# Rounded-weight products of gate and up first, remainder products behind them, in a transformer kernel

## The chip, the cores and the metric

One core of a Trainium2 chip runs the whole program. The metric is the device time of one execution in microseconds (us), the median of three runs. TensorE (PE in the profile, PEld for its weight loads) multiplies, VectorE (DVE) and ScalarE (ACT) work on tiles, GpSimd (POOL) does small things, SyncE (SP) issues nearly all DMAs. The engines have one instruction stream each and wait for one another on semaphores.

## The reference, cut to what matters

The reference is a chain of two transformer stacks of two layers each over 256 tokens of width 1024, all in float32. Between attention parts it has six feed-forward blocks (one in each layer of the first stack, two in each layer of the second), all of this form, with a hidden width of 2816:

```
def swiglu(x, wg, wu, wd):
    return (jax.nn.silu(x @ wg) * (x @ wu)) @ wd
```

## The kernel before, in words

Every weight matrix is read from memory in units of 1 MB (128 partitions by 2048 float32). There are three buffers of each kind, so unit u uses buffer u mod 3. For each unit SP fills `raw` (L562), ACT writes the rounded weights `w_hi` (`split_hi`, L761) and counts `hi_ready`, DVE writes what rounding lost, `w_lo = raw - w_hi` (`split_lo`, L1178), and counts `lo_ready`. A product in nearly full precision is then made of products with `w_hi` and with `w_lo`. When PE is done with a unit it counts `unit_used`; ACT may write `w_hi` of unit u+3 only when unit u is counted, and SP may refill `raw` when `w_lo` of its former unit is written.

A feed-forward block (`ffn`, f = 0 to 5) works through 11 groups of 256 hidden columns. Each group has three units: gate (G), up (U) and down (D). For a gate or an up unit PE runs `wide` (L1992): 16 matmuls of 512 columns with rounded weights (`rounded`, L2006; both halves of the split activations at once), then 16 of 256 columns with the remainders (`remainder`, L2010), into a pair of PSUM banks, G_B for gate and U_B for up. A down unit (`down`, L2043) is 24 matmuls of 512 columns (helper `three`, L1907 to L1909) into four other banks. PE's order is G, U of group g+1, then D of group g; only at the end of a block D9 and D10 stand one right behind the other, behind U10.

What ACT and DVE do with a group, in their order in a steady group (`group` L862, and DVE's `gates` and `group` around L1241 to L1262):

- ACT: `split_hi` of the down unit; `split_hi` of the next gate unit (waits for G counted); `gate_sum` copy of half of G_B (L861); silu (L868); `up_sum` copy of half of U_B (L870, waits for U counted); `hid_hi` (L872, the rounded hidden values); `split_hi` of the next up unit.
- DVE: `split_lo` of the down unit; `gate_sum` addition (L1238, after which G_B is free); multiplication of the gate sums (L1246); `split_lo` of the next gate unit; `up_sum` addition (L1253, after which U_B is free); product `hid` (L1257); `hid_lo` (L1260, what rounding of the hidden values lost); `split_lo` of the next up unit.

PE's D of group g waits for `hid_lo` of group g (`hidden_lo`). In the last group the place of the next gate unit is taken by unit D10, the place of the next up unit by the first unit of the next stage (unit 33 of the block), and the second unit of the next stage (34) follows. The last block loads none of those two.

Behind a block stands either an addition to x in halves by DVE (`add_ffn`, L1613; blocks 2, 3 and 4), then transposes on PE that wait for it (`turn_piece`, L1880); or a norm with squares on ACT, products on DVE (L1589, L1228) and transposes (L1896; blocks 0 and 1); or the final norm (block 5). L1866 are matmuls without use, which only keep PE busy. The first group of a block is made by `wide_first` and `wide` called directly; `gate_up` makes groups 1 to 10.

The diff touches `gate_up` alone.

Of the kernel before, what the change touches and what calls it, by code (L numbers as in the profile page):

```python
# [29 lines left out]
KC = D // P  # L30
# [210 lines left out]
def build(nc, a, noted):  # L241

    with ExitStack() as ctx:
# [91 lines left out]
        G_B, U_B, ACC = pair[0], pair[1], bank[4:8]  # L335
# [87 lines left out]
        def sem(name):  # L423
            return ctx.enter_context(nc.semaphore(name))

        def sig(name):
# [3 lines left out]
        hi_ready, lo_ready, unit_used = sem("hi_ready"), sem("lo_ready"), sem("unit_used")  # L430
# [3 lines left out]
        gate_cross, up_cross, gate_summed, up_summed = (  # L434
            sem(n) for n in ("gate_cross", "up_cross", "gate_summed", "up_summed"))
# [87 lines left out]
        def hi_half(which, c):  # L523
            return which[:, 2 * SEQ * c:2 * SEQ * c + SEQ]
# [1337 lines left out]
        def _(pe):  # L1862
# [120 lines left out]
            def ffn(f, pieces):  # L1983
                u0 = ffns[f][0]
                base = NG * f

                def split_weights(u):

                    s = u % RING
                    return [v[s][:, :].rearrange("p (c n) -> p c n", c=KC) for v in (w_hi, w_lo)]  # L1990

                def wide(u, i, out):  # L1992

                    pe.wait_ge(hi_ready, u + 1 + 6 * i)
                    w = split_weights(u)
                    for c in range(KC):
                        for m in range(2):
                            rounded(w, out, m, c)
                    pe.wait_ge(lo_ready, u + 1 + 6 * i)
                    for c in range(KC):  # L2000
                        for m in range(2):
                            last = remainder(w, out, m, c)
                    return last

                def rounded(w, out, m, c):
                    pe.matmul(out[:, 512 * m:512 * (m + 1)], w[0][:, c, P * m:P * (m + 1)],  # L2006
                              xt[:, 2 * SEQ * c:2 * SEQ * (c + 1)], start=(c == 0), stop=False)

                def remainder(w, out, m, c):
                    return pe.matmul(out[:, 512 * m + SEQ:512 * (m + 1)], w[1][:, c, P * m:P * (m + 1)],  # L2010
                                     hi_half(xt, c), start=False, stop=(c == KC - 1))
# [23 lines left out]

                def gate_up(u, i, g):

                    pe.wait_ge(gate_summed, base + g)
                    wide(u, i, G_B).then_inc(unit_used, 1)
                    pe.wait_ge(up_summed, base + g)  # L2040
                    wide(u + 1, i, U_B).then_inc(unit_used, 1)

                def down(u, i, g, p, first, last_group):  # L2043
                    s = u % RING
# [22 lines left out]
                pe.matmul(ACC[0][:, 0:SEQ], ones[:, :], rstd_diag, start=True, stop=True)\  # L2067
                  .then_inc(small_mm.sem, small_mm.mark(("rstd rows", f)))
                gate_up(u0 + 2, 0, 1)
                pe.wait_ge(prep_ready.sem, prep_ready.at(("rstd rows", f)))  # L2070
                down(u0 + 4, 0, 0, 0, True, False)
                with pe.Fori(0, 4) as i:
                    for j in range(2):
                        gate_up(u0 + 5 + 3 * j, i, 2 * i + j + 2)
                        down(u0 + 7 + 3 * j, i, 2 * i + j + 1, 1 - j, False, False)
                gate_up(u0 + 29, 0, 10)
                down(u0 + 31, 0, 9, 1, False, False)
                down(u0 + 32, 0, 10, 0, False, True)
# [186 lines left out]
            u = 0  # L2265
# [192 lines left out]
```

## Time and profile before

| | |
|---|---|
| median of 3 runs | 1627.94 us (1627.82 to 1628.86) |
| profiled execution | 1628.18 us, of which the span of the program 1626.3 us |
| granted clock of TensorE | 0.999 of full |
| PE busy | 1602.4 us (99%) |
| PE weight loads busy | 1362.1 us (84%) |
| DVE busy | 1068.3 us (66%) |
| ACT busy | 881.3 us (54%) |
| POOL busy | 85.4 us (5%) |
| mean DMA rate | 166 GB/s |

A time in the trace is counted from the start of the span. A line of the timeline has the start, the duration, engine and line of the code, operation, output and inputs, the number of merged instructions, and in brackets how long the engine sat idle before it and what ended that. A matmul's duration (390 ns at 512 columns) is longer than the distance to the next one (227 ns), because matmuls overlap; so 16 of them that start 227 ns apart take 3.79 us from the first start to the last end.

### The profile page before, as it was taken

What the parts mean: (1) busy time and instruction counts of PE and PEld (TensorE: products, weight loads), DVE (VectorE), ACT (ScalarE), POOL (GpSimd) and SP (SyncE); (2) the same over time, 40 slices, a digit from 0 to 9 for tenths busy, and PEclk for the clock granted to TensorE, in tenths of its full rate; (3) what the DMA queues carried; (4) which work ended last, traced back from release to release, by engine and by line L of the source; (5) the groups of instructions that cost most, each with busy time, mean ns of one, the idle gap of its engine ahead of it and who ended that gap; (6) DMA issues with size and microseconds to landing.
All of it is one profiled execution on the core that took longest, in us unless ns stands there. A gap on an engine that the chain in (4) does not pass through costs nothing.

```text
span 1626.3 us, 23915 instructions
## 1 busy us (share of the span) xinstructions
PE 1602.4 (99%) x9386; PEld 1362.1 (84%) x9386; DVE 1068.3 (66%) x1323; ACT 881.3 (54%) x1306; POOL 85.4 (5%) x160
## 2 busy tenths in 40 slices
PE   9999999999999999999999999999999999999998
PEld 8778888876888888888987788888888888788887
DVE  6766666786765676656758566666666666766665
ACT  6755444675554555444557454445544556654444
POOL 1000000030000030000002000002000001000000
PEclk9999999999999999999999999999999999999999
DMA  8325555524555557565430355557655542055552
GB/s 282 130 78 205 188 184 192 186 80 142 182 187 200 181 179 251 181 204 183 156 130 2 128 197 183 193 181 219 218 182 192 172 156 79 2 191 199 182 191 91
DMA packets 197098, 270.62 MB, mean 166 GB/s; under 512 B 4856, under 2 KB 165232, under 8 KB 197024
## 3 DMA queue, kind: packets, MB, share of 16 engines
q1 hardware_dynamic: 194016, 262.08, 47.6%
q0 software_dynamic: 2544, 7.09, 1.7%
q8 instruction: 50, 0.82, 0.2%
q10 hardware_dynamic: 464, 0.44, 0.1%
q14 instruction: 24, 0.20, 0.0%
HBM read 268.53 MB, written 1.05 MB: 166 GB/s over the span
## 4 chain that ended last, share of the span: by engine, by line
PE 89%; DVE 5%; ACT 2%; POOL 1%; issue 1%; DMA 0%; POOLq 0%; SPq 0%; DVEq 0%; ACTq 0%
PE pair L2006 30%; PE pair L2010 16%; PE bank L1907 10%; PE bank L1908 10%; PE bank L1909 10%; PE bank L1976 4%; PE pair L1907 1%; PE pair L1909 1%; PE pair L1908 1%; PE bank L2212 1%; POOL blk L640 1%; PE pair L2161 1%; PE bank L2182 1%; DVE probs L1355 1%; DVE w_lo L1178 1%
## 5 line engine op out<-in xcount | busy, mean ns | idle before, releaser
L1178 DVE TENSOR_TENSOR w_lo<-raw,w_hi 128x2048 fp32r<-128x2048 f32 (+1 forms) x246 | 560.8, 2281 | 137.5 <-ACT w_hi L761 136.3
L761 ACT ACTIVATE w_hi<-raw 128x2048 fp32r<-128x2048 f32 (+1 forms) x247 | 470.1, 1907 | 273.0 <-PE pair L2010 191.5
L2006 PE MATMUL pair<-xt,w_hi 128*128 128x512 f32 x2112 | 507.1, 391 | 0.7 <-DVE xt L1198 0.2
L2006 PEld LDWEIGHTS pair<-xt,w_hi 128*128 128x128 f32 x2112 | 390.6, 188 | 78.9 <-issue 1.8
L2010 PEld LDWEIGHTS pair<-xt,w_lo 128*128 128x128 f32 x2112 | 273.2, 191 | 11.8
L2010 PE MATMUL pair<-xt,w_lo 128*128 128x256 f32 x2112 | 276.8, 283 | 0.0
L1907 PE MATMUL bank<-w_hi,hid_hi 128*128 128x512 f32 x528 | 206.2, 390 | 0.0
L1908 PE MATMUL bank<-w_hi,hid_lo 128*128 128x512 f32 x528 | 206.1, 390 | 0.0
L1909 PE MATMUL bank<-w_lo,hid_hi 128*128 128x512 f32 x528 | 205.4, 389 | 0.0
L1238 DVE TENSOR_TENSOR gate_sum<-pair,gate_sum 128x512 f32<-128x512 f32 x66 | 45.6, 691 | 199.6 <-ACT gate_sum L861 199.6
L1909 PEld LDWEIGHTS bank<-w_lo,hid_hi 128*128 128x128 f32 x528 | 99.1, 188 | 21.1
L1907 PEld LDWEIGHTS bank<-w_hi,hid_hi 128*128 128x128 f32 x528 | 99.4, 188 | 19.0
L1908 PEld LDWEIGHTS bank<-w_hi,hid_lo 128*128 128x128 f32 x528 | 99.4, 188 | 18.3
L1907 PE MATMUL bank<-w_hi,xt 128*128 128x256 f32 (+1 forms) x352 | 108.4, 308 | 0.4 <-DVE xt L1198 0.4
L1908 PE MATMUL bank<-w_hi,xt 128*128 128x256 f32 (+1 forms) x352 | 106.5, 302 | 0.0
L1909 PE MATMUL bank<-w_lo,xt 128*128 128x256 f32 (+1 forms) x352 | 106.4, 302 | 0.0
L868 ACT ACTIVATE act_g<-hid 128x512 f32<-128x512 f32 x66 | 41.8, 633 | 112.5 <-DVE hid L1246 112.5
L872 ACT ACTIVATE hid_hi<-hid 128x512 fp32r<-128x512 f32 x66 | 41.7, 632 | 106.5 <-DVE hid L1257 106.5
L1260 DVE TENSOR_TENSOR hid_lo<-hid,hid_hi 128x512 fp32r<-128x512 f32 x66 | 45.7, 693 | 46.1 <-ACT hid_hi L872 46.1
L917 ACT ACTIVATE probs<-pair,negmax 128x256 f32<-128x256 f32 (+1 forms) x168 | 72.7, 472 | 2.5 <-DVE negmax L1327 1.4
L616 POOL TENSOR_SCALAR sumsq<-sumsq 128x2 f32<-128x2 f32 (+3 forms) x31 | 8.8, 283 | 1241.7 <-ACT junk L777 649.9
L1907 PEld LDWEIGHTS bank<-w_hi,xt 128*128 128x128 f32 x352 | 67.1, 191 | 5.1 <-issue 2.7
(294 smaller groups left out, 1738.1 us busy)
## 6 DMA issues: line engine op xcount, KB each, us to landing
raw<-in_w_gate_up SPq DMA_DIRECT2D x44, 1024.0 KB, 5.1
raw<-in_ffn_wg SPq DMA_DIRECT2D x44, 1024.0 KB, 5.1
raw<-in_ffn_wu SPq DMA_DIRECT2D x44, 1024.0 KB, 5.2
raw<-in_ffn_wd SPq DMA_DIRECT2D x44, 1024.0 KB, 4.9
raw<-in_w_in SPq DMA_DIRECT2D x26, 1024.0 KB, 5.1
raw<-in_w_down SPq DMA_DIRECT2D x22, 1024.0 KB, 5.0
raw<-in_w_o SPq DMA_DIRECT2D x8, 1024.0 KB, 5.0
raw<-in_w_out SPq DMA_DIRECT2D x8, 1024.0 KB, 5.0
```

The lines of the kernel that those rows point to most:

```text
L761: act.activation(w_hi[s][:, 0:filled(u)], raw[s][:, 0:filled(u)], ACT.Copy).then_inc(hi_ready, 1)
L868: act.activation(act_g[p][:, :], hid[p][:, :], ACT.Silu).then_inc(silu_ready, 1)
L917: act.activation(probs[n % 3][:, 512 * u + lo:512 * u + lo + w], S_B[n % 2][:, 512 * u + lo:512 * u + lo + w], ACT.Exp, bias=negmax[:, c:c ...
L1178: dve.tensor_tensor(w_lo[s][:, 0:filled(u)], raw[s][:, 0:filled(u)], w_hi[s][:, 0:filled(u)].bitcast(F32), ALU.subtract)\
L1238: dve.tensor_tensor(by_m(gate_sum[p]), main_half(G_B), by_m(gate_sum[p]), ALU.add)\
L1260: dve.tensor_tensor(hid_lo[p][:, :], hid[p][:, :], hid_hi[p][:, :].bitcast(F32), ALU.subtract).then_inc(hidden_lo, 1)
L1907: pe.matmul(out, hi, w_h, start=first, stop=False)
L1908: pe.matmul(out, lo, w_h, start=False, stop=False)
L1909: return pe.matmul(out, hi, w_l, start=False, stop=last)
L1976: last = pe.matmul(group_bank(g, t)[:, 0:n], xt_chunk(t, x_part(xt, 4 * r + c)), w_part[s][:, n * c:n * (c + 1)], start=(r == 0 and c == 0 ...
L2006: pe.matmul(out[:, 512 * m:512 * (m + 1)], w[0][:, c, P * m:P * (m + 1)], xt[:, 2 * SEQ * c:2 * SEQ * (c + 1)], start=(c == 0), stop=False)
L2010: return pe.matmul(out[:, 512 * m + SEQ:512 * (m + 1)], w[1][:, c, P * m:P * (m + 1)], hi_half(xt, c), start=False, stop=(c == KC - 1))
```

## The change

`gate_up` no longer calls `wide` for gate and then for up. It makes gate's 16 rounded products, up's 16 rounded products, gate's 16 remainder products and up's 16 remainder products. Each wait stands ahead of the part that needs it: the up unit's two waits, for `up_summed` (U_B free) and for `hi_ready`, now stand in front of gate's remainder products. `unit_used` is counted after gate's and after up's remainder products, so in the same order as before. Instructions, operands and results are the same ones.

```diff
                 def gate_up(u, i, g):
 
-                    pe.wait_ge(gate_summed, base + g)
-                    wide(u, i, G_B).then_inc(unit_used, 1)
-                    pe.wait_ge(up_summed, base + g)
-                    wide(u + 1, i, U_B).then_inc(unit_used, 1)
+                    for k, out, summed in ((0, G_B, gate_summed), (1, U_B, up_summed)):
+                        pe.wait_ge(summed, base + g)
+                        pe.wait_ge(hi_ready, u + k + 1 + 6 * i)
+                        w = split_weights(u + k)
+                        for c in range(KC):
+                            for m in range(2):
+                                rounded(w, out, m, c)
+                    for k, out in ((0, G_B), (1, U_B)):
+                        pe.wait_ge(lo_ready, u + k + 1 + 6 * i)
+                        w = split_weights(u + k)
+                        for c in range(KC):
+                            for m in range(2):
+                                last = remainder(w, out, m, c)
+                        last.then_inc(unit_used, 1)
```

## Rows read from the trace of the kernel before

**Rows 1.** The page: the start of part 1, and the chain by engine

```profile
PE 1602.4 (99%) x9386; PEld 1362.1 (84%) x9386; DVE 1068.3 (66%) x1323; ACT 881.3 (54%) x1306; POOL 85.4 (5%) x160
...
PE 89%; DVE 5%; ACT 2%; POOL 1%; issue 1%; DMA 0%; POOLq 0%; SPq 0%; DVEq 0%; ACTq 0%
```

**Rows 2.** PE's waits, largest total (total us, times, longest)

```profile
PE bank L2212 <- DVE xt L1402: 3.0, 6, 1.0
```

**Rows 3.** Timeline of a group in the middle of block 0

```profile
163.16 3.79 PE L2006 MATMUL pair<-xt,w_hi 128*128 128x512 f32 x16
...
166.79 2.08 PE L2010 MATMUL pair<-xt,w_lo 128*128 128x256 f32 x16
...
168.90 1.92 ACT L761 ACTIVATE w_hi<-raw 128x2048 fp32r<-128x2048 f32 x1 [3.62 <-PE pair L2010]
...
172.36 2.08 PE L2010 MATMUL pair<-xt,w_lo 128*128 128x256 f32 x16
...
177.16 1.90 ACT L761 ACTIVATE w_hi<-raw 128x2048 fp32r<-128x2048 f32 x1
...
179.51 3.59 PEld L2006 LDWEIGHTS pair<-xt,w_hi 128*128 128x128 f32 x16
179.74 3.79 PE L2006 MATMUL pair<-xt,w_hi 128*128 128x512 f32 x16
```

**Rows 4.** Timeline of the last group (10) of block 0

```profile
282.80 2.08 PE L2010 MATMUL pair<-xt,w_lo 128*128 128x256 f32 x16
...
284.98 1.92 ACT L761 ACTIVATE w_hi<-raw 128x2048 fp32r<-128x2048 f32 x1 [3.62 <-PE pair L2010]
...
288.37 2.08 PE L2010 MATMUL pair<-xt,w_lo 128*128 128x256 f32 x16
288.74 2.28 DVE L1178 TENSOR_TENSOR w_lo<-raw,w_hi 128x2048 fp32r<-128x2048 f32 x1
288.86 0.63 ACT L868 ACTIVATE act_g<-hid 128x512 f32<-128x512 f32 x1 [1.48 <-DVE hid L1246]
...
290.48 0.60 ACT L870 ACTIVATE up_sum<-pair 128x512 f32<-128x512 f32 x1 [0.99 <-PE pair L2010]
...
293.30 0.69 DVE L1260 TENSOR_TENSOR hid_lo<-hid,hid_hi 128x512 fp32r<-128x512 f32 x1 [0.70 <-ACT hid_hi L872]
...
295.75 0.39 PE L1907 MATMUL bank<-w_hi,hid_hi 128*128 128x512 f32 x1
```

**Rows 5.** Timeline of group 1 of block 0, DVE

```profile
140.12 2.29 DVE L1178 TENSOR_TENSOR w_lo<-raw,w_hi 128x2048 fp32r<-128x2048 f32 x1
...
142.32 0.68 DVE L1253 TENSOR_TENSOR up_sum<-pair,up_sum 128x512 f32<-128x512 f32 x1
...
144.50 0.69 DVE L1260 TENSOR_TENSOR hid_lo<-hid,hid_hi 128x512 fp32r<-128x512 f32 x1 [0.70 <-ACT hid_hi L872]
```

**Rows 6.** Timeline of the start of group 1 of block 0

```profile
132.51 0.69 DVE L1253 TENSOR_TENSOR up_sum<-pair,up_sum 128x512 f32<-128x512 f32 x1 [1.18 <-ACT up_sum L870]
...
133.42 1.73 PEld L2010 LDWEIGHTS pair<-xt,w_lo 128*128 128x128 f32 x13
```

**Rows 7.** Timeline of the end of block 2

```profile
770.42 0.69 DVE L1260 TENSOR_TENSOR hid_lo<-hid,hid_hi 128x512 fp32r<-128x512 f32 x1 [0.70 <-ACT hid_hi L872]
...
772.22 2.29 DVE L1178 TENSOR_TENSOR w_lo<-raw,w_hi 128x2048 fp32r<-128x2048 f32 x1 [1.11 <-ACT w_hi L761]
...
775.09 2.29 DVE L1178 TENSOR_TENSOR w_lo<-raw,w_hi 128x2048 fp32r<-128x2048 f32 x1 [0.57 <-ACT w_hi L761]
...
777.29 2.72 DVE L1613 SCALAR_TENSOR_TENSOR x<-bank,half_rstd,x 128x512 f32<-128x512 f32 x4
...
778.75 1.09 PE L1880 MATMUL pair<-cst,x 128*128 128x128 f32 x8 [0.28 <-DVE x L1613]
```

**Rows 8.** Timeline of the first 12 us, matmuls without use

```profile
3.33 3.17 PE L1866 MATMUL bank<-ones 128*128 128x128 f32 x14
...
8.49 2.84 PE L1866 MATMUL bank<-ones 128*128 128x128 f32 x24
```

## The prediction, made before the changed kernel was run

> **What bounds the kernel now.** I read the page first, then PE's waits, then the timeline of one steady group, then those of the block's first and last group, since a change of order can only matter where somebody waits. PE is busy for 1602.4 of 1626.3 us and holds 89% of the chain that ended last [rows 1]. Its largest wait in sum is 3.0 us and belongs to the attention part [rows 2]; no wait in the list has its end in the middle of a feed-forward block. So the matmul stream is the bound there, and a change can win only by making that stream shorter, and can lose by holding it up. DVE (66%) and ACT (54%) have room on average, but both work through lists in a fixed order, and what counts is when each entry gets done.
>
> The stream's price in a steady group: 16 rounded products occupy 166.79 - 163.16 = 3.63 us of starts (227 ns each), and the next group begins 179.74 - 163.16 = 16.58 us after this one [rows 3]. Gate's remainders start at 3.63, up's at 9.20, so up's rounded ones start at 9.20 - 3.63 = 5.57 and 16 remainders take 1.92 us. G is done at 5.71 (166.79 + 2.08 - 163.16), U at 11.28 (172.36 + 2.08 - 163.16), D runs from 9.20 + 1.92, near 11.1, on.
>
> **The stream itself: nothing.** The same 64 matmuls run. Before there are three changes of length inside G and U (long, short, long, short), afterwards one. The distance from gate's first to up's first remainder is 172.36 - 166.79 = 5.57 us [rows 3], and 16 x 0.227 + 16 x 0.120 is 5.55; so a change of length costs at most 0.02 us. If both that go away saved 0.01 us each, 60 calls of `gate_up` would give 1.2 us; if the new order costs as much, the same with the other sign. I take 0, since the two runs' own prices already add up to the measured distance within 0.02.
>
> **What moves.** G is counted used 3.63 us later (9.34 instead of 5.71 after the group's start), U at the same time. Up's rounded products start at 3.63 instead of 5.57, so U_B and up's `w_hi` are needed 1.94 us earlier. Remainders are needed later or, for up, hardly changed. Everything that hangs on G moves by 3.63: ACT's next L761, `gate_sum`, DVE's next L1178, silu. What hangs on U starts from the same time but stands behind those in both queues.
>
> **Steady groups: nothing, by cover.** Relative to the group's start: ACT's L761 for the next gate goes from 5.74 to 9.37 and ends at 11.29; DVE's L1178 for that unit, which starts 3.8 us after ACT's L761 did (288.74 - 284.98 = 3.76 [rows 4]), runs from 13.1 to 15.4. Then `up_sum`, `hid`, `hid_hi` and `hid_lo` follow, 2.78 us from the end of that L1178 to the end of `hid_lo` when DVE is the late one (145.19 - 142.41 [rows 5]). So `hid_lo` ends at 18.2 (needed by D, whose turn is at 27.7) and `up_sum` at 16.1 (needed at 20.2). `hid_lo` starts right behind `hid_hi`, so that ends near 17.5, and ACT's L761 for the next up unit follows it, 1.90 us [rows 3], to 19.3. PE's weight load for up's first rounded product is due at 16.58 + 3.63 - 0.23 = 19.98 (weight loads run 0.23 ahead, 179.51 against 179.74 [rows 3]). Margin 0.68 us; before it was 16.58 + 5.57 - 0.23 - 15.90 = 6.0, 15.90 being 177.16 + 1.90 - 163.16. This is the tightest of the steady waits: if ACT's chain were x us longer than 0.68, each of 9 groups in 6 blocks would lose x. SP's refills move with DVE's L1178 by at most 3.63 us and their data are needed over 9 us later; nothing is queued behind them that is needed sooner. In group 1 `up_sum` of group 0 ends at 132.51 + 0.69 = 133.20, and up's first weight load now comes where gate's first remainder load was, 133.42 [rows 6]: margin 0.22 us, six times in the kernel.
>
> **The last group of each block: here the cover is gone.** D9 hides the making of the last hidden values, and D10 follows it. Before: G10 ends at 282.80 + 2.08 = 284.88, U10 at 288.37 + 2.08 = 290.45, `hid_lo` at 293.30 + 0.69 = 293.99, and PE's D10 starts at 295.75 [rows 4]; 1.76 us to spare. After: G10 ends at 288.51. ACT's L761 (for D10), `gate_sum`, DVE's two steps and DVE's L1178 form a rigid chain behind it; L1178 ended at 288.74 + 2.28 = 291.02 and now ends at 294.65. Silu's end moves from 289.49 to 293.12, ACT's L870 (0.60) behind it ends near 293.7 instead of 291.08, still ahead of DVE, which is in L1178. Then the 2.78 us of [rows 5]: `hid_lo` ends at 297.43, 3.44 us later. The matmul that waits starts between 0.05 us (L1880 at 778.75 behind the second L1613, which ends near 778.70 [rows 7]) and that plus the 0.23 of a weight load behind it; a weight load with its matmul waits here, so I take 0.23. That is 297.66 instead of 295.75: 1.91 us lost. For six blocks 11.5 us.
>
> **Behind blocks 2, 3 and 4 there is more.** DVE's L1178 for unit 33 ends 3.41 us after `hid_lo` (772.22 + 2.29 = 774.51 against 771.11), that for unit 34 ended at 777.38, and the four L1613 follow it without a break; PE's transposes already wait for them [rows 7]. After (U10 ends at 767.56, which is 3.55 ahead of `hid_lo`'s end as in block 0, 293.99 - 290.45 = 3.54): `hid_lo` at +6.98 (as 297.43 - 290.45), the first L1178 at +10.38, the second right behind it (2.29 less an overlap of 0.09, as L1613 at 777.29 starts before 777.38) at +12.58, instead of 777.38 - 767.56 = +9.82. L1613 and with it the transposes move by 2.76, so these three blocks lose 0.85 us more each, 2.6 us. In block 0, DVE moves as much, but PE has the next stage's first projection between D10 and the transposes; blocks 1 and 5 have no second L1178 there. Bounds of this term: 0 and 3 x 0.85.
>
> **Sum.** 3 x 1.91 + 3 x 2.76 = 14.0 us; the profiled execution of 1628.18 us (span 1626.3) would be 1642.2, and since it lies 0.24 above the median, the forecast is 1641.9, 0.86% slower.
>
> **Rivals.** (1) Not slower: the push is hidden by D9. The gate's side of the group had 1.76 us to spare in front of D10 [rows 4], and if what hangs on U (L870, `up_sum`, `hid`) did not have to stand behind what hangs on G, `hid_lo` would end near 293.99 as before and the time would be 1628. It decides at a push of 1.76 us; I work out 3.44. For it: U10 ends when it did. Against it: in group 1 DVE's `up_sum` began at 142.32 without any idle time in front of it, when the L1178 ahead of it ended [rows 5], so DVE keeps its order. A sentence of the Trainium skill bears on this: its page "TensorE: Matmul & The Clock Gate", section "Architectural detail: the array is 16× 32×32, not 1× 128×128", says that ACT and DVE are strict first-in first-out and only PE takes weight loads ahead. By that rule rival 1 falls and the sum stays 14.0; row and rule agree. Chance 0.05.
> (2) The margin of 0.68 us in steady groups is used up, by ACT or DVE waiting on counts in more places than I see. At 0.3 us lost in each of 54 groups it costs 16 us more, 1658. For it: the small margin. Against it: the steady groups repeat to 0.02 us. Chance 0.05.
> (3) The clock falls in the new idle stretch before D10. At the kernel's start 14 matmuls took 3.17 us, later 24 took 2.84 [rows 8], 227 against 118 ns each: half speed. The slow stretch there lasted to 6.50 us at least, so a fall of that length would cost half of it, 3.3 us, six times: 20 us on top, 1662. Against it: PE has single waits of 1.0 us [rows 2] with the granted clock at 0.999 of 2.4 GHz over the whole run; the new ones are about 1.7 us. [...] Chance 0.04.
> (4) Faster: the two changes of length that go away are worth more than the tail costs. It needs 14.0 / 120 = 0.12 us each and the rows give at most 0.01; it decides at 0.12. Time at 0.15 each: 1624. Chance 0.01.
>
> **Chances and range.** My forecast 0.85: slower by 0.7 to 1.1%. Its own range goes from 1639 (tails alone, without the extra in blocks 2 to 4, 11.5 us) to 1646 (the small margin of group 1 or the ends of blocks 0 and 1 costing another 0.6 us each block). The range I give is 1638 to 1647; rivals 1, 2, 3 and 4 with 0.15 together lie outside. About 0.2% is what a measurement here can tell from no change. Slower 0.94 (forecast, rivals 2 and 3), same 0.05, faster 0.01.
>
> **What would show it.** In the profile after: a wait of PE at D10 on DVE `hid_lo` L1260, six times, near 1.7 us; no wait on L761 or L1253 in L2006; steady groups still 16.58 us apart; matmul distances of 227 and 120 ns; PE's L1880 waiting about 1 us at three blocks; PE busy unchanged. I am wrong if `hid_lo` of group 10 ends less than 5.3 us after U10, if PE waits within steady groups, or if the clock's share falls.

## The result

The changed kernel takes 1641.36 us (median of 6 runs, 1641.08 to 1641.64) against 1628.05 us (median of 6 runs) before: 13.3 us or 0.8% longer, ratio 1.0081 with a 95% interval of 1.0071 to 1.0090. Its profiled span is 1639.2 us against 1626.3, at the same granted clock of 0.999.

The page of the changed kernel, the start of its part 1, its chain by engine, and the group of part 5 for the first matmul of a down unit (busy us, mean ns, idle before it, what ended that):

```profile
PE 1602.1 (98%) x9386; PEld 1361.0 (83%) x9386; DVE 1057.8 (65%) x1323; ACT 868.3 (53%) x1306; POOL 85.4 (5%) x160
...
PE 86%; DVE 8%; ACT 3%; POOL 1%; issue 1%; DMA 0%; POOLq 0%; DVEq 0%; SPq 0%; ACTq 0%
...
L1907 PE MATMUL bank<-w_hi,hid_hi 128*128 128x512 f32 x528 | 206.7, 391 | 10.1 <-DVE hid_lo L1260 10.1
```

PE does the same work in the same time as in [rows 1]; DVE and ACT took over 4% of the chain. Where they did so is told by PE's waits (total us, times, longest), to be held against [rows 2], where no wait in the middle of a feed-forward block stood in the list:

```profile
PE bank L1907 <- DVE hid_lo L1260: 10.1, 6, 1.7
PE pair L1880 <- DVE x L1613: 4.1, 6, 1.1
PE bank L2222 <- DVE xt L1402: 3.0, 6, 1.0
```

The first is new: six waits of 1.7 us, one in each block. The second, behind blocks 2, 3 and 4, was 1.5 us in six waits in the kernel before:

```profile
PE pair L1880 <- DVE x L1613: 1.5, 6, 0.3
```

The timeline of the last group of block 0, the counterpart of [rows 4] (start, duration, engine, line; x is how many instructions are merged):

```profile
286.04 4.00 PE L2010 MATMUL pair<-xt,w_lo 128*128 128x256 f32 x32
...
288.21 1.92 ACT L761 ACTIVATE w_hi<-raw 128x2048 fp32r<-128x2048 f32 x1 [4.89 <-PE pair L2010]
290.04 0.57 ACT L861 ACTIVATE gate_sum<-pair 128x512 f32<-128x512 f32 x1
...
291.98 2.28 DVE L1178 TENSOR_TENSOR w_lo<-raw,w_hi 128x2048 fp32r<-128x2048 f32 x1
...
292.63 0.58 ACT L870 ACTIVATE up_sum<-pair 128x512 f32<-128x512 f32 x1
294.18 0.68 DVE L1253 TENSOR_TENSOR up_sum<-pair,up_sum 128x512 f32<-128x512 f32 x1
...
296.35 0.69 DVE L1260 TENSOR_TENSOR hid_lo<-hid,hid_hi 128x512 fp32r<-128x512 f32 x1 [0.69 <-ACT hid_hi L872]
...
297.16 0.19 PEld L1907 LDWEIGHTS bank<-w_hi,hid_hi 128*128 128x128 f32 x1 [2.08 <-issue]
297.19 0.47 PE L1907 MATMUL bank<-w_hi,hid_hi 128*128 128x512 f32 x1 [1.69 <-DVE hid_lo L1260]
```

U10 ends at 290.04, `hid_lo` at 297.04, 7.00 us later (before 3.54), and D10 starts 7.15 us after U10 instead of 5.30. `up_sum` (L1253) has its ACT half ready at 293.21 and starts at 294.18, when L1178 ends.

The end of block 2, the counterpart of [rows 7]:

```profile
778.80 4.49 DVE L1178 TENSOR_TENSOR w_lo<-raw,w_hi 128x2048 fp32r<-128x2048 f32 x2 [1.11 <-ACT w_hi L761]
...
783.21 2.72 DVE L1613 SCALAR_TENSOR_TENSOR x<-bank,half_rstd,x 128x512 f32<-128x512 f32 x4
784.66 0.86 PEld L1880 LDWEIGHTS pair<-cst,x 128*128 128x128 f32 x8 [1.53 <-DVE x L1613]
784.67 1.09 PE L1880 MATMUL pair<-cst,x 128*128 128x128 f32 x8 [1.11 <-DVE x L1613]
```

Both L1178 now run back to back and end at 783.29, and PE's transposes wait 1.11 us for the addition instead of 0.28. A steady group, the counterpart of [rows 3]:

```profile
162.91 7.42 PE L2006 MATMUL pair<-xt,w_hi 128*128 128x512 f32 x32
...
179.47 4.70 PE L2006 MATMUL pair<-xt,w_hi 128*128 128x512 f32 x20
...
180.29 1.90 ACT L761 ACTIVATE w_hi<-raw 128x2048 fp32r<-128x2048 f32 x1
```

32 rounded products stand in one run. The next group starts 16.56 us later (16.553 by the unrounded starts; 16.573 before), and ACT's L761 for the next up unit ends at 182.19, 2.72 us into that group. There is no wait of PE in it.

By the distances of PE's unrounded starts, span against span: D10 starts 1.85 us later (5.305 us after U10 before, 7.156 now) and its stream takes 0.10 us more, in six blocks 11.7 us; the way from D10 to the next feed-forward block is 0.81 to 0.86 us longer behind blocks 2, 3 and 4, 2.5 us; 60 groups are 0.020 us shorter, -1.2 us; the stretch ahead of the first block is 0.2 us shorter. Together 12.8 us; the spans differ by 12.83.

### The profile page after: what moved, and what is told of

Read it like the earlier page. It is cut to its first block, busy times and chain, and to the rows that moved or that the text cites. A ratio compares the mean times of both kernels' runs of the same rounds, so it can differ in the third digit from the quotient of the medians.

```text
span 1639.2 us, 23915 instructions
## 1 busy us (share of the span) xinstructions
PE 1602.1 (98%) x9386; PEld 1361.0 (83%) x9386; DVE 1057.8 (65%) x1323; ACT 868.3 (53%) x1306; POOL 85.4 (5%) x160
## 4 chain that ended last, share of the span: by engine, by line
PE 86%; DVE 8%; ACT 3%; POOL 1%; issue 1%; DMA 0%; POOLq 0%; DVEq 0%; SPq 0%; ACTq 0%
PE pair L2006 29%; PE pair L2010 15%; PE bank L1907 9%; PE bank L1908 9%; PE bank L1909 9%; PE bank L1976 4%; DVE w_lo L1178 2%; ACT w_hi L761 1%; PE pair L2171 1%; PE bank L2222 1%; PE pair L1907 1%; POOL blk L640 1%; PE bank L2192 1%; PE pair L1909 1%; PE pair L1908 1%
## 5 line engine op out<-in xcount | busy, mean ns | idle before, releaser
L761 ACT ACTIVATE w_hi<-raw 128x2048 fp32r<-128x2048 f32 (+1 forms) x247 | 463.7, 1901 | 306.4 <-PE pair L2010 277.6
L1178 DVE TENSOR_TENSOR w_lo<-raw,w_hi 128x2048 fp32r<-128x2048 f32 (+1 forms) x246 | 555.4, 2279 | 108.7 <-ACT w_hi L761 107.7
L2006 PE MATMUL pair<-xt,w_hi 128*128 128x512 f32 x2112 | 495.8, 390 | 0.7 <-DVE xt L1198 0.2
L2010 PEld LDWEIGHTS pair<-xt,w_lo 128*128 128x128 f32 x2112 | 265.3, 191 | 7.2
L2010 PE MATMUL pair<-xt,w_lo 128*128 128x256 f32 x2112 | 267.4, 283 | 0.0
L1260 DVE TENSOR_TENSOR hid_lo<-hid,hid_hi 128x512 fp32r<-128x512 f32 x66 | 45.7, 693 | 46.1 <-ACT hid_hi L872 46.1
```

Source lines behind the costliest of these rows:

```text
L761: act.activation(w_hi[s][:, 0:filled(u)], raw[s][:, 0:filled(u)], ACT.Copy).then_inc(hi_ready, 1)
L1178: dve.tensor_tensor(w_lo[s][:, 0:filled(u)], raw[s][:, 0:filled(u)], w_hi[s][:, 0:filled(u)].bitcast(F32), ALU.subtract)\
L1260: dve.tensor_tensor(hid_lo[p][:, :], hid[p][:, :], hid_hi[p][:, :].bitcast(F32), ALU.subtract).then_inc(hidden_lo, 1)
```

## The experiments

My theory: all of the loss arises in the last group of each block, where the hidden values have only D9 to hide behind, and each group in the new order makes the stream 0.020 us shorter. Its rivals stand with each run.

**Group 10 in the former order.**

```diff
-                gate_up(u0 + 29, 0, 10)
+                gate_up_apart(u0 + 29, 0, 10)
```

`gate_up_apart` has the former body: gate whole, then up whole.

> The changed kernel, but group 10 of each block in the former order (gate whole, then up whole). My theory (the loss is made by the last group alone, and each group in the new order saves 0.020 us of stream): no wait of PE on L1260, 54 groups save 0.020 each, 1628.05 - 1.1 = 1627.0 us. Rival A (ACT's and DVE's lists run later from group to group and the last group only shows it): about 1641 us, with the wait on L1260 still there. Rival B (no saving in the stream, the 0.02 us a group is something else): 1628.05.

Measured: 1627.02 us (11 runs), ratio 0.9992 (0.9983 to 1.0001). No wait on L1260 is left; D10 starts 5.30 us after U10 again, and nine groups take 149.21 us instead of 149.39 in every block. Rival A falls, and by those 0.18 us in every block rival B as well. By the time alone the gain of 1.0 to 1.2 us is at the edge of what can be measured; it is the trace that shows it.

**Only group 10 in the new order.**

```diff
-                gate_up(u0 + 29, 0, 10)
+                gate_up_together(u0 + 29, 0, 10)
```

This is an edit of the kernel before; `gate_up_together` has the new body.

> The kernel before, but group 10 of each block in the new order. My theory: the whole loss and none of the saving but that of six groups: 6 x 1.96 + 3 x 0.83 - 0.1 = 14.1, 1642.2 us. Rival A (lists running late over ten groups): near 1628, since only one group is changed.

Measured: 1642.29 us, ratio 1.0087 (1.0072 to 1.0102). Six calls out of 60 carry the whole loss. Without the other 54 the time is 0.9 us longer than that of the changed kernel (1.1 by the profiled spans, as 54 times 0.020 would give), a difference near what the spread of the executions allows one to see.

**Less push: 8 and 12 of up's rounded products ahead of gate's remainders.**

```
                    ...
                    for m, c in places[:n]:
                        rounded(wu, U_B, m, c)
                    pe.wait_ge(lo_ready, u + 1 + 6 * i)
                    for m, c in places:
                        last = remainder(wg, G_B, m, c)
                    last.then_inc(unit_used, 1)
                    for m, c in places[n:]:
                        rounded(wu, U_B, m, c)
                    ...
```

This is the middle of a new helper that makes group 10 alone; gate's rounded products stand ahead of it, up's remainders behind it. n is 8 or 12.

> The changed kernel, but in group 10 only 8 of up's 16 rounded products stand in front of gate's remainders, the other 8 behind them. Gate is done 1.81 us later than before the change instead of 3.63. My theory (1.76 us of slack in front of D10, then each us of push costs one): hid_lo ends 5.16 us after U10, D10 starts at most 0.2 us late; blocks 2 to 4 still lose about 0.9 each to the addition behind DVE's second L1178. 1628.05 - 1.1 + 0.6 + 2.7 = 1630.2 us. Rival (no slack, loss proportional to the push): half of 14.3, 1634.

> The same with 12 of up's rounded products in front of gate's remainders, push 2.72 us. My theory: hid_lo ends 6.07 us after U10, D10 starts 0.92 late and its stream 0.1 more; blocks 2 to 4 lose 1.85 in all: 1628.05 - 1.1 + 3 x 1.02 + 3 x 1.85 = 1635.6 us. Rival (proportional to the push): 1637.7.

Measured: 1630.34 us with 8 (ratio 1.0013, 1.0004 to 1.0023) and 1636.06 us with 12 (1.0049, 1.0033 to 1.0064). The table gives the distances by the starts and ends in the traces, the same in all six blocks within 0.02 us.

| rounded products of up ahead of gate's remainders | gate counted later by | U10's end to `hid_lo`'s end | U10's end to D10's start | time |
|---|---|---|---|---|
| 0 (former order in group 10) | 0 | 3.55 | 5.30 | 1627.02 |
| 8 | 1.81 | 5.18 | 5.33 | 1630.34 |
| 12 | 2.72 | 6.10 | 6.25 | 1636.06 |
| 16 (changed kernel) | 3.63 | 7.01 | 7.16 | 1641.36 |

By the unrounded starts, the first 1.8 us of push cost D10's start 0.02 us (and its stream, which then began behind a short idle stretch, 0.1 as in the changed kernel), the next 0.91 cost 0.92 and the last 0.91 cost 0.91. That is a slack used up and then one for one, not a share of the push. In the kernel with 8, PE's waits have no L1260 any more, but the addition is late all the same:

```profile
PE pair L1880 <- DVE x L1613: 4.1, 6, 1.2
```

Here the two terms of the sum are seen apart: L1613 stands behind both L1178 and feels a push that D10 does not.

**D10's remainders made behind the hidden values.**

```diff
                 gates(10, 0)
-                split_lo(u0 + 32)
                 group(10, 0)
+                split_lo(u0 + 32)
```

> The changed kernel, but in group 10 DVE's L1178 for unit D10 stands behind hid_lo (L1260) instead of in front of the up_sum addition. My theory (both the hidden values and D10's remainders are due at D10, and DVE has to do both after G10): hid_lo ends about 6.1 us after U10 instead of 7.0, but L1178 ends at 8.3, and D10 waits for that: 1.3 us more in blocks 0, 1 and 5, about 0.35 more in blocks 2 to 4, 1646 us. Rival (the position of L1178 in the list is what costs, the hidden values alone are what D10 waits for): D10 0.9 us earlier, 1636 us.

Measured: 1652.4 us (1651.33 to 1655.31), ratio 1.0154 (1.0138 to 1.0171), slower than either theory says. The timeline of block 0:

```profile
293.85 0.69 DVE L1253 TENSOR_TENSOR up_sum<-pair,up_sum 128x512 f32<-128x512 f32 x1 [1.18 <-ACT up_sum L870]
...
296.03 0.69 DVE L1260 TENSOR_TENSOR hid_lo<-hid,hid_hi 128x512 fp32r<-128x512 f32 x1 [0.70 <-ACT hid_hi L872]
296.64 4.49 DVE L1178 TENSOR_TENSOR w_lo<-raw,w_hi 128x2048 fp32r<-128x2048 f32 x2
...
298.98 0.19 PEld L1907 LDWEIGHTS bank<-w_hi,hid_hi 128*128 128x128 f32 x1 [3.30 <-DVE w_lo L1178]
298.98 0.50 PE L1907 MATMUL bank<-w_hi,hid_hi 128*128 128x512 f32 x1 [2.88 <-DVE w_lo L1178]
```

`hid_lo` is 0.9 us earlier relative to U10 (6.09 instead of 7.01), but PE waits for L1178, and D10 starts 8.34 us after U10: the rival falls. DVE has to finish both before D10, and with L1178 moved away it stands idle for 1.18 us in front of `up_sum`, which L1178 had filled. The run also splits the delay of `hid_lo`: of 3.46 us (7.01 against 3.55) L1178's place accounts for 0.92. The other 2.54 us came with L1178 out of the way, so they came down the rest of the chain behind G, in which ACT's L761 for D10, `gate_sum` and silu stand ahead of the `up_sum` copy; no run moved anything in ACT's list there.

Six times 1.18 us is 7.1; behind blocks 2 to 4 D10 now ends late enough for the first half of the addition to be done, which gives back 1.16, 1.33 and 1.16, together 3.7. The rest is the clock. By stretches around D10 of blocks 0 to 5 (stretch, its length, busy time and count of PE, PEld, DVE, ACT and POOL, then PEclk, the granted share of the clock, the DMAs' share and GB/s):

```profile
298.00:305.00 7.00, 6.02 (x28) 5.03 (x29) 6.90 (x6) 3.33 (x6) 0.65 (x2) 1.00 0.67 235
589.00:596.00 7.00, 6.43 (x32) 5.46 (x33) 4.89 (x7) 3.33 (x6) 0.74 (x2) 1.00 0.78 247
782.00:790.00 8.00, 7.90 (x31) 6.42 (x32) 6.38 (x6) 0.81 (x2) 0.00 (x0) 0.79 0.90 283
1113.90:1122.00 8.10, 7.95 (x32) 6.34 (x32) 6.74 (x7) 1.17 (x3) 0.00 (x0) 0.82 0.87 275
1303.60:1311.60 8.00, 7.84 (x31) 6.36 (x32) 6.38 (x6) 0.81 (x2) 0.00 (x0) 0.79 0.89 281
1635.60:1643.60 8.00, 7.34 (x24) 5.61 (x24) 4.68 (x8) 2.52 (x7) 1.21 (x4) 0.79 0.00 0
```

In blocks 2 to 5 part of the stretch ran at 1.2 instead of 2.4 GHz, behind an idle stretch of 2.9 us, and the 24 matmuls of D10 took 7.1 to 7.3 us instead of 5.75: four times 1.3 to 1.6, 6.1 us. 1641.4 + 7.1 - 3.7 + 6.1 is 1650.9, near the fastest run of this kernel, which is the profiled one. The granted clock of its four runs was 0.995, 0.994, 0.994 and 0.992 at 1651.33, 1652.19, 1652.62 and 1655.31 us, so the spread goes with the clock; in which blocks the other three lost it, nothing shows. In blocks 0 and 1 the same idle stretch left the clock at 1.00. The waits of 1.7 us in the changed kernel never moved it. This is rival 3 of the prediction, at an idle stretch that the change itself does not reach, and at 1.3 to 1.6 us for each fall instead of 3.3. The Trainium skill, page "TensorE: Matmul & The Clock Gate", section "Why this matters for your kernels", warns that an idle gap between bursts of matmuls, once it is long enough, drops the clock to its lower level. Four of the six idle stretches of 2.9 us here agree; the other two did not drop it.

**The addition ahead of unit 34's remainders, behind blocks 2, 3 and 4.**

```diff
-                    if f != 1:
+                    if f == 0:
                         split_lo(u0 + 34)
...
                 add_ffn(2 + 2 * l, ("mix2", l))
                 turn_lo(("mix2", l), 10 + 3 * l)
+                split_lo(u + 1)
```

(and the same call behind the `turn_lo` that follows block 3, where the condition `if l == 0` goes)

> The changed kernel, but behind blocks 2, 3 and 4 DVE adds to x (L1613) and makes the halves of x (L1198) first and then L1178 of unit 34. My theory (these blocks lose 0.83 us each because the addition stands behind that L1178): PE's wait on L1613 falls from about 1.1 to about 0.4 us, 3 x 0.83 = 2.5 less, 1638.9 us; PE's wait on L1260 unchanged. Rival (the transposes wait for D10's end anyway): 1641.4 us.

> Both edits: group 10 in the former order, and the addition in front of L1178 of unit 34 behind blocks 2 to 4. My theory: 1627.0 less at most 0.1 for each of the three blocks, since the addition's second half waits for D10's end anyway: 1626.7 us. Rival (the addition was bound by L1178 before the change too, by 0.4 us): 1625.8.

Measured: 1637.89 us (ratio 1.0060, 1.0044 to 1.0076) for this edit on the changed kernel, and 1625.85 us (11 runs, ratio 0.9986, 0.9977 to 0.9996) together with the former order in group 10. The first was to gain 2.5 us and gained 3.5, the second was to gain at most 0.3 on 1627.02 and gained 1.2. In the traces the way from D10 to the next feed-forward block became 1.16, 1.33 and 1.18 us shorter behind the three blocks in the first, and 0.30, 0.49 and 0.35 us shorter in the second. So the mechanism stands, but "the addition's second half waits for D10's end anyway" was no reason. The timeline of the kernel with both edits shows why:

```profile
777.70 1.04 PE L1880 MATMUL pair<-cst,x 128*128 128x128 f32 x8
778.33 1.57 ACT L790 ACTIVATE xt<-pair,gains_t 128x256 fp32r<-128x256 f32 x4 [3.91 <-PE pair L1880]
779.22 2.19 DVE L1198 SCALAR_TENSOR_TENSOR xt<-pair,gains_t,xt 128x256 fp32r<-128x256 f32 x5
779.36 0.86 PEld L1880 LDWEIGHTS pair<-cst,x 128*128 128x128 f32 x8 [0.87 <-DVE x L1613]
```

The first eight transposes need only the addition's first half and now follow D10 without a wait; ACT and DVE then make those parts of x while PE waits for the other half. The next stage starts on the chunks in turn, so the first half's time counts too: without this edit, with group 10 in the former order, the last transpose behind block 2 starts 2.80 us after D10's last matmul and the next stage 3.25 us after it; here it is 2.72 and 2.78. This kernel is faster than both; of the 1.2 us against the one with the former order in group 10 its trace shows 1.1.

**The same stream with more changes of length.**

```diff
-                    for c in range(KC):
+                    for half in range(2):
+                        for c in range(4 * half, 4 * half + 4):
```

> The kernel before, with each gate and up unit made in two halves: 8 rounded products, 8 remainders, 8 rounded, 8 remainders. No wait and no matmul more; 126 units have one pair of changes of length more. My theory (the first five long matmuls behind a short run stand 27 ns further apart in sum, the first two short ones behind a long run 7 ns closer): 126 x 0.020 = 2.5 us, 1630.6 us. Rival (the saving of the new order comes from the waits that it puts elsewhere): 1628.05.

Measured: 1630.37 us (11 runs), ratio 1.0014 (1.0005 to 1.0023). A steady group takes 16.613 us instead of 16.573, 0.020 for each pair of changes added. By the starts in its trace, the first five 512-column matmuls behind a run of short ones stand 233, 236, 228, 232 and 231 ns apart on average instead of 227, and the first two 256-column ones behind a run of long ones 113 and 119 instead of 120. The saving belongs to the lengths and not to where the waits stand. Why the matrix engine needs five long matmuls to get back to 227 ns, no run here shows.

**How thin the steady groups' margin is.** Both kernels have the new order with the former one in group 10; `again` is 1 or 2 in groups 2 to 9 and 0 elsewhere.

```diff
+                    for n in range(again):
+                        act.activation(junk[:, 512 * n:512 * (n + 1)], hid[p][:, :], ACT.Copy)
                     act.activation(hid_hi[p][:, :], hid[p][:, :], ACT.Copy).then_inc(hidden_hi, 1)
```

> The new order with group 10 in the former one (1627.0 us), and in groups 2 to 9 of each block ACT copies hid once more, to a tile that nobody reads, right before hid_hi (0.63 us, 0.54 with its overlap); the results stay as they are. My theory (in a steady group up's rounded weights are ready 0.68 us before PE loads the first of them): 0.14 us of that are left, no wait, 1627.0 us. Rival (the margin is smaller than I read it, or counts take longer to arrive): each hundredth of a us missing costs 0.5 us, so above 1628.

> The same with two copies more (1.08 us). My theory: 0.40 us missing in each of 48 groups, and 0.05 to 0.1 for the first matmul behind an idle stretch: PE waits for ACT's L761 in front of up's rounded products, 1649 us. Rival (ACT is idle for almost half of the time and takes it up): 1627.0 us.

Measured: 1627.29 us with one copy (ratio 0.9995, 0.9985 to 1.0004) and 1642.06 us with two (1.0086, 1.0069 to 1.0102). So 0.54 us more on ACT are all but free (by the starts block 3 alone takes 0.25 us longer, the others nothing) and 1.08 cost 15.0 us. The step is where I put it, its size is not: by the starts a group takes 16.885 us instead of 16.553, 0.33 and not 0.45, and only groups 3 to 9 do, 42 and not 48, since the copies of group g delay group g+1 and group 10 stands in the former order. That is 14.0 us; block 3 loses 0.8 us more, and the cause of that is open. The timeline with two copies:

```profile
183.04 0.19 PEld L2008 LDWEIGHTS pair<-xt,w_hi 128*128 128x128 f32 x1
...
183.68 0.30 PEld L2008 LDWEIGHTS pair<-xt,w_hi 128*128 128x128 f32 x2 [0.46 <-ACT w_hi L761]
```

The weight load comes 0.42 us late (due 0.23 behind the one at 183.04), but a matmul that finds PE empty starts with its weight load instead of 0.23 behind it; that returns part of the delay, and the next distance of 337 ns takes some back. 0.42 - 0.22 + 0.11 + 0.02 for the distances behind it is the 0.33.

## Why the prediction was right

1641.9 us was forecast, 1641.36 measured; 0.86% against 0.81%, with 1638 to 1647 as the range. The place, the cause and the way were forecast; that the time agrees to 0.5 us is in part luck, since the terms miss by 1.0 us together (see the sum).

- **What bounds.** Right. The matmul stream is the bound, and it lost only where it was held up.
- **The stream itself.** The sign was there, the size was set to 0. The bound of 1.2 us was exactly the saving: 60 calls, one pair of changes of length less in each, 0.020 us a pair. The measured distance of 5.57 us against 5.55 from the runs' prices was the pair's price, and I read it as rounding. This is the largest miss of the sum.
- **Steady groups hidden.** Right, with no wait in them. L761 for up's weights ended 182.19 - 179.47 = 2.72 us into the group; 19.3 - 16.58 = 2.7 was worked out. The run with 0.54 us more on ACT shows the margin, the run with 1.08 its end. The margin of 0.22 us in group 1 held too: gate's last rounded product and up's first start 227 ns apart in all six blocks.
- **The last group.** The chain was forecast to 0.02 us: `hid_lo` at U10 + 6.98, measured 7.00 to 7.01. D10's start moved by 1.85 and its stream grew by 0.10, together 1.95 instead of 1.91. Two misses all but cancel there: D10 starts 0.15 us behind `hid_lo`'s end and not 0.23, and the longer stream was not in the sum. The four doses show that a slack of 1.8 us of push went first.
- **Behind blocks 2 to 4.** 0.85 us each forecast, 0.81 to 0.86 measured. The term was right; what I said later of its state before the change (nothing to gain) was not.
- **Sum.** 11.7 + 2.5 - 1.2 is 13.0 by these terms against a forecast of 14.0. The profiled executions differ by 12.9 and the medians by 13.3, so the spread of the executions brought the time nearer to the forecast than the terms are.
- **Rivals.** (1) hidden by D9: shown wrong by the new wait, and by the doses, which show that D9 hides 1.8 us and no more; DVE's `up_sum` started when L1178 ended, not when its input was there. (2) margin used up: not by this change, but by 1.08 us more work. (3) the clock: not at waits of 1.7 us, yes in four blocks of six at 2.9 us, at 1.3 to 1.6 us each and not 3.3. (4) faster: the mechanism exists, with a tenth of the price that it would have needed.

## What to carry to other kernels

When PE is the bound, a change of its order is priced first at the places where the next work has least to hide behind. Here that was the last iteration; the steady ones began to cost only when their margin was used up. Count for every queue what stands between the moved signal and the waiting instruction, in that queue's order; the slack before is used first, then each microsecond costs one. If the reordering pays in the steady groups and costs at the end, keep it for the steady groups only (here that is worth 1.0 to 1.2 us of 1628), and look at what other work stands in a queue ahead of something that is waited for.

## What the runs showed of the hardware that was not expected

A short matmul run costs its successor: five distances of 233, 236, 228, 232 and 231 ns instead of 227 behind 256-column matmuls, 0.020 us a pair of changes net, by the kernels with one pair fewer in a group and with one more in a unit. A matmul behind an idle stretch starts within 0.03 us of its weight load instead of 0.23 behind it, and the stream after it is about 0.10 us longer (5.70 instead of 5.60 us for D10), with 0.31 us instead of 0.23 to the second matmul. Idle stretches of 2.9 us dropped the granted clock in four of six blocks, those of 1.7 us in none of six, in the changed kernel, with the addition moved, and with only the last group changed.
